# Removing the last eight drain pauses from TensorE's stream in a two-block transformer kernel

## The reference, cut to what matters

```python
proj = h @ w_in[l]                      # 2048 x 6656 (+16)
mk, mv = jnp.split(m @ w_mem_kv[l], 2)  # 2048 x 1024
x = x + mixed @ w_out[l]                # 2048 x 2048
...
proj = h @ w_in_2                       # 2048 x 10240 (+8)
merged = (sigmoid(g_a) * (o_a @ w_branch_a) + sigmoid(g_b) * (o_b @ w_branch_b)) @ w_out_2
q = h @ w_query                         # 2048 x 2048
act = gelu(h @ expert_u.T)              # 2048 x 16384
out = (gates * act) @ expert_v          # 16384 x 2048
```

## Time and profile before

| what | value |
|---|---|
| device time, 3 runs | 2878.76, 2884.63, 2885.59 us; median 2884.63 us |
| the profiled execution's own time | 2897.16 us |
| its span, first to last instruction | 2895.4 us |
| mean granted TensorE clock | 0.990 of full |
| TensorE matmuls busy | 2819.8 us, 97%, 24173 matmuls |
| GpSimd busy | 2287.4 us, 79% |
| ScalarE busy | 1311.2 us, 45% |
| VectorE busy | 1098.4 us, 38% |

### The profile page before, as it was taken

The page is one execution under the profiler, slowest core; times in us unless marked ns, Lnnn a source line. Parts: engine busy times, 40 slices in busy tenths (PEclk is TensorE's granted clock), DMA queues, the critical chain, the costliest instruction groups (busy, mean ns, idle before and its releaser), DMA issues.

```text
span 2895.4 us, 58383 instructions
## 1 busy us (share of the span) xinstructions
PE 2819.8 (97%) x24173; PEld 2796.8 (97%) x24173; DVE 1098.4 (38%) x1556; ACT 1311.2 (45%) x1545; POOL 2287.4 (79%) x925
## 2 busy tenths in 40 slices
PE   7999988999999999999999999999999999999998
PEld 7999988899999999999999999999999999999998
DVE  6103356335232251334697771502205041044322
ACT  6354462554443344444545664443434444344333
POOL 6877740389776799888785558999999899899996
PEclk9999989999999999999999999999999999999999
DMA  6544420155444455565454556565565655655653
GB/s 250 175 162 171 169 88 15 59 174 193 171 167 140 159 190 202 178 214 189 160 186 177 219 219 219 186 231 191 194 227 185 226 184 201 222 203 207 228 196 122
DMA packets 85846, 524.64 MB, mean 181 GB/s; under 512 B 8672, under 2 KB 23136, under 8 KB 24544
## 3 DMA queue, kind: packets, MB, share of 16 engines
q1 hardware_dynamic: 68400, 489.38, 48.0%
q10 hardware_dynamic: 17328, 33.56, 3.1%
HBM read 504.03 MB, written 18.87 MB: 181 GB/s over the span
## 4 chain that ended last, share of the span: by engine, by line
PE 76%; issue 12%; POOL 10%; DVE 1%; ACT 0%; POOLq 0%; DVEq 0%; ACTq 0%
PE banks L1450 76%; POOL wlo L407 10%; PE banks L1559 0%; DVE T L854 0%; DVE dec L1043 0%; DVE ycv L997 0%; DVE gv L1014 0%; DVE gv L1016 0%; POOLq L406 0%; DVE hid_lower L1421 0%; DVE picks L1360 0%; DVE at__96 L1051 0%; DVE qkv L1007 0%; ACT whi L430 0%; POOLq L401 0%
## 5 line engine op out<-in xcount | busy, mean ns | idle before, releaser
L407 POOL TENSOR_TENSOR wlo<-raw,whi 128x1024 fp32r<-128x1024 f32 x920 | 2282.7, 2504 | 557.6 <-ACT whi L430 554.6
L430 ACT ACTIVATE whi<-raw 128x1024 fp32r<-128x1024 f32 x920 | 961.5, 1058 | 894.2 <-PE banks L1450 886.1
L1450 PE MATMUL banks<-xhi,whi 128*128 128x256 f32 x4672 | 639.8, 280 | 10.4 <-ACT xhi L532 4.2
L1450 PE MATMUL banks<-xhi,wlo 128*128 128x256 f32 x4672 | 634.4, 278 | 3.6 <-POOL wlo L407 3.6
L1450 PE MATMUL banks<-xlo,whi 128*128 128x256 f32 x4672 | 636.2, 279 | 0.0
L1450 PEld LDWEIGHTS banks<-xhi,whi 128*128 128x128 f32 x4672 | 582.6, 189 | 12.7 <-issue 8.2
L1450 PEld LDWEIGHTS banks<-xhi,wlo 128*128 128x128 f32 x4672 | 581.7, 189 | 4.4 <-POOL wlo L407 4.4
L1450 PEld LDWEIGHTS banks<-xlo,whi 128*128 128x128 f32 x4672 | 583.0, 189 | 1.0
L922 DVE TENSOR_TENSOR X<-banks,X 128x256 f32 (+1 forms) x112 | 47.5, 424 | 700.0 <-PE banks L1450 700.0
L1450 PE MATMUL banks<-hid_lower,whi 128*128 128x256 f32 x2048 | 273.8, 276 | 0.0
L1450 PEld LDWEIGHTS banks<-hid_lower,whi 128*128 128x128 f32 x2048 | 251.1, 188 | 0.0
(11 more groups left out here) (369 smaller groups left out, 2319.6 us busy)
## 6 DMA issues: line engine op xcount, KB each, us to landing
raw<-in_w_exp SPq DMA_DIRECT2D x256, 1024.0 KB, 4.8
raw<-in_w_in SPq DMA_DIRECT2D x132, 1024.0 KB, 4.9
raw<-in_w_out SPq DMA_DIRECT2D x32, 1024.0 KB, 4.8
raw<-in_w_br SPq DMA_DIRECT2D x16, 1024.0 KB, 4.9
raw<-in_w_q SPq DMA_DIRECT2D x16, 1024.0 KB, 4.8
gates<-gst ACTq DMA_DIRECT2D x16, 1024.0 KB, 4.5
gch<-gates ACTq DMA_DIRECT2D x7, 2048.0 KB, 13.2
raw<-in_w_kv SPq DMA_DIRECT2D x8, 1024.0 KB, 9.7
```

The costliest lines, as they stand in the source:

```text
L407: pool.tensor_tensor(wlo[:, s, :, :], raw[:, j, h * HALF:(h + 1) * HALF, :], whi[:, s, :, :].bitcast(F32), ALU.subtract).then_inc(lo_ready, 1)
L430: act.activation(whi[:, (2 * j + h) % 4, :, :], raw[:, j, h * HALF:(h + 1) * HALF, :], ACT.Copy).then_inc(hi_ready, 1)
L1450: return nc.tensor.matmul(o, lhsT, rhs, start=start, stop=stop, **k)
```

## The change

The tuple of paused units becomes empty. `pause` is then never called, the semaphore `beat` is neither signalled nor awaited, and nothing else differs: the same matmuls in the same order, the same weight loads, the same waits between engines.

```diff
@@ -57,7 +57,7 @@
 N_MEM, N_X, N_X1, N_X3, N_OUT = range(5)
-PAUSED = (29, 49, 53, 57, 61, 133, 189, 205)
+PAUSED = ()
 L_MEM, L_X, L_MIXED, L_IN2, L_ATT, L_MERGED, L_EXP = range(7)
```

## The result

The changed kernel is slower: ratio 1.0076 to the kernel before, 95% interval 1.0053 to 1.0100. The median of all twelve of its runs is 2919.28 us, against 2884.27 us for the kernel before on the same occasions; the forecast was 2884.0 us with a range of 2871 to 2899.

The account below looks back on a forecast made before the run. TensorE's stream bounds the kernel, at a fast or slow pace. The terms +1.6 - 3.3 + 11.3 - 0.2 - 4.8 - 5.2 give -0.6 us, taking the median 2884.6 to 2884.0 us, range 2871 to 2899.

Parts of the forecast that it names:

- The pauses themselves: All eight paused groups of eight matmuls: each loses a 0.20 us pause on TensorE's path, 1.6 us gained in all.
- Units 29 to 57: Units 29, 49, 53, 57, slow before the pause and fast after: without it the fast pace is lost, +1.6 us net.
- Unit 133: Slow before its pause, fast after: without it 54.8 units, to unit 187, stay slow, +11.3 us.
- Rival 2: The stream arrives fast at unit 133, so the loss behind it does not come: 2872.5 us, chance 0.18.
- Units 61, 189 and 205: Without pauses, stretches behind 61 and 205 become fast, -3.3 and -4.8 us; 189, slow on both sides, gives -0.2 us.
- -5.2 for 227 to 251: Units behind the wait at 1544 us, slow now, restart fast: between 0 and -5.2 us, taken as -5.2.
- the terms are small differences of pace and carry over, if the paces there are those of the profile: The -0.6 us summed on the profiled execution (2897.2 us) is applied to the runs' median, 12.5 us lower.
- Small work acts as before, whatever the entry: The next small work behind each pause leaves the pace as in the trace of before, whatever pace enters it.
- rival 3: Loss behind 133 comes, units 76 to 101 turn slow (+5.5 us), 227 to 251 stay slow: 2894.7 us, chance 0.14.
- rival 4: The long stretch, units 252 to 459, restarts at the slow pace: 43.7 us lost, 2927.7 us, chance 0.12.
- The wait for `picks`: TensorE's 5.72 us wait for VectorE at 1544 us moves with TensorE and stays near 5.7, so the 4.8 us gain remains.
- The clock: Idle times could lower the granted clock; the change adds none, so nothing is counted, with a bound of 3.4 us.

## Why the prediction was wrong

- *The pauses themselves, 1.6 us.* Right in size: groups of 1.30 us became 1.10.
- *Units 29 to 57, +1.6 us.* Right in the profiles for 30, 31, 50, 51, 54 and 55. In all three profiles of the changed kernel the stream came slow up to unit 56 and went on fast from there, so 58 and 59 lost nothing: a quarter of the term fell away.
- *Unit 133, +11.3 us.* Right: 11.0 us by the runs that take out only this pause, 11.5 us for units 133 to 187 between the two profiled executions, and slow in every profile without it. Rival 2 never occurred.
- *Units 61, 189 and 205, -3.3, -0.2 and -4.8 us, and -5.2 for 227 to 251.* This is where the sum failed. The step was "the terms are small differences of pace and carry over, if the paces there are those of the profile". They need not be. The profile that I read was of kind 1, in which the pauses of 61 and 205 slow the stream and 189 does nothing, and its units 227 to 251 were slow, as in only 3 of 13 profiles. The timed runs beside it lay 12.5 us lower, and that was the sign: with -3.3 for 61, -3.4 for 189, and -10 for 205 and what follows, 2897.2 becomes 2880.5 us, near where most of them are. In runs of kind 2 taking out 61 and 205 gains only the pauses, 0.4 us, and taking out 189 costs 16 x 0.21 - 0.2 = 3.2. The sum is then 1.6 - 0.2 + 11.3 + 3.2 - 0.2 = +15.7 us; the lower group moved by 16.5. This account was fitted afterwards and isn't shown: no profile of the kernel before is of kind 2. The nearest is the one with 21 pauses, 2887.9 us, which less 2.6 us for its thirteen more gives an estimate of 2885.3. On chip B, where the second profile of the kernel before is of kind 1 too, the change cost 2 to 4 us in the lower group, near the +4.6 that my own sum gives without its last term, which I had called little better than even.
- *"Small work acts as before, whatever the entry"*, called the weakest step, failed where it was tested: in the profile after, the key scores ahead of unit 204 were entered slow and left slow, where before they were entered slow and left fast, and the 4.8 us at 206 to 226 did not come in it. In the second and third profile they did. And in the third, units 77 to 92 were slow behind a fast entry (749 matmuls in the 88 us from 650 to 738; 779 in the first), as rival 3 feared. So small work doesn't act the same way in each execution, even on the same entry.
- *The long stretch.* I gave it 0.12 as rival 4, with the argument that three runs within 6.8 us showed a steady restart. Three were too few: 2 of 12 of the same kernel lay in the upper group, and 5 of 11 of the changed one. Its price was right (43.7 us forecast, 42 between the groups).
- *The wait for `picks`* stayed at 5.72 us and moved with TensorE, as worked out. *The clock* was judged by a profile in which it happened not to fall ahead of unit 252. In the 7.5 us around the start of unit 252 the granted clock reads 0.54 to 0.77 in ten of the thirteen profiles of this layout, 0.77 in the profile after, and 1.00 in three; the two levels are 1.2 and 2.4 GHz, so 0.77 costs 7.5 x 0.23 = 1.7 us (an estimate). It does not choose the pace: where it fell unit 252 went on fast in seven and slow in three, where it did not, fast in two and slow in one.

That the pace is handed on in this way, that pauses turn it, and what the units cost at either pace was right. Wrong was to take one profile's paces for those of the median run, and to hold the restart, which can end at either pace, for settled. Open: what makes an execution of kind 1 or 2, and whether the eight pauses, which stand 200 us and more ahead of the long stretch, lower the chance of its slow pace. The counts (9 of 29 against 4 of 58 side by side, 16 of 106 for the kernel before over all its runs) speak for it, but the share differs from chip to chip, 1 of 35 on B and 3 of 7 on E; with only 133 it is 6 of 25.

## What to carry to other kernels

When a profiled execution lies further from the median of the timed runs than those lie from each other, the difference is a finding: look for a state that differs before you carry small terms from one to the other. Count instructions per stretch, not busy time, to see the pace of a pipelined engine. A fix that works by disturbing a stream is only as good as the state that it meets: the pauses at the long stretch did no harm in one kind of execution, and the one at 253 turned the whole stretch slow in the other, so measure it on several occasions, and look for the cause (here the layout of the operands in memory changes the paces, though none of the seven others tried was faster).

## What the runs showed of the hardware

- One stream of loads and matmuls of one form has two stable pitches, 113.3 and 117.8 ns, at a granted clock of 1.00, and keeps either for over 1100 us. Waits, pauses of 0.2 us and small work between decide which.
- The pitch depends on where the weights start relative to the moving data, modulo 1024 bytes: 113.3 or 117.8 ns at 64, 448 and 576 bytes, 118.3 at 32, 117.3 to 118.7 at 608, 118.7 to 120.0 at 640, 120.0 at 0 and 256. From 0 to 64 bytes that is up to 5.6% of TensorE's time. Distance and absolute start weren't told apart.
- The same program (21 pauses) answers its pauses in one of two ways: entered fast, all 16 left fast in one profile, both left slow in another. Over eight profiles none mixes the two answers (11 of 11 left slow in six, 17 of 17 left fast in two).
